# Norm and head scales spread from a step-zero stationary column, and some rounding moved to ScalarE, in a two-layer hybrid diffusion backbone

## What is computed

```python
hx = modulate(rmsnorm(x, g_norm1[l]), mod_x[0], mod_x[1])
px = split_cols(hx @ w_in[l])
...
x = x + mod_x[2] * (jnp.concatenate([m_x, d_x, c_x], axis=-1) @ w_out[l])
...
x = x + mod_x[5] * ffn(modulate(rmsnorm(x, g_norm2[l]), mod_x[3], mod_x[4]))
```

## Time and profile before

| | us |
|---|---|
| median of three runs | 1443.08 |
| the profiled execution, its own time | 1440.16 |
| its span, first to last instruction | 1438.2 |
| TensorE busy | 1376.3 (96%) |
| VectorE busy | 980.4 (68%) |
| ScalarE busy | 629.1 (44%) |
| GpSimd busy | 188.2 (13%) |

### The profile page before, as it was taken

One profiled execution on the slowest core, in us unless ns is written; L12 is line 12 of the kernel. 1 busy time (PEld: TensorE's weight loads), 2 busy tenths in 40 slices (PEclk: granted clock), 3 DMA queues, 4 the chain that ended last, 5 costly groups with the idle time before them and its releaser, 6 DMA issues.

```text
span 1438.2 us, 20655 instructions
## 1 busy us (share of the span) xinstructions
PE 1376.3 (96%) x7782; PEld 1132.2 (79%) x7782; DVE 980.4 (68%) x1470; ACT 629.1 (44%) x993; POOL 188.2 (13%) x136
## 2 busy tenths in 40 slices
PE   6999999989999999999999989798999999999996
PEld 4878787667788888888879887587888888888885
DVE  3756886764644443353468696568898898898896
ACT  3434334642310110010035434646767767777674
POOL 0039980000000000000003960000000000000000
PEclk9999999989999999999999999899999999999998
DMA  9344443412422232232334223439977977977940
GB/s 397 139 176 175 176 176 118 176 59 92 155 105 88 91 115 88 81 110 85 120 118 147 90 87 118 175 133 420 379 284 296 370 278 301 359 297 299 359 163 30
DMA packets 30882, 267.08 MB, mean 186 GB/s; under 512 B 3424, under 2 KB 3552, under 8 KB 4960
## 3 DMA queue, kind: packets, MB, share of 16 engines
q1 hardware_dynamic: 30816, 266.16, 48.6%
HBM read 265.09 MB, written 1.05 MB: 185 GB/s over the span
## 4 chain that ended last, share of the span: by engine, by line
PE 80%; DVE 10%; ACT 4%; issue 3%; DMA 3%; SPq 0%; DVEq 0%; ACTq 0%
PE ps L552 37%; PE ps L1052 17%; PE ps L1072 7%; PE ps L889 3%; PE ps L574 3%; PE ps L739 2%; DMA sb_arena<-mod 2%; PE ps L778 2%; PE ps L797 1%; PE ps L559 1%; DVE sb_egu_lo L2140 1%; DVE sb_h_lo L1622 1%; DVE sb_h_hi L1621 1%; PE ps L788 1%; DVE sb_ew_lo L2152 1%
## 5 line engine op out<-in xcount | busy, mean ns | idle before, releaser
L552 PE MATMUL ps<-sb_h_hi,sb_w_hi 128*128 128x512 f32 (+1 forms) x640 | 241.2, 377 | 2.6 <-DVE sb_w_lo L1636 1.1
L552 PE MATMUL ps<-sb_h_hi,sb_w_lo 128*128 128x512 f32 (+1 forms) x640 | 239.0, 373 | 0.0
L552 PE MATMUL ps<-sb_h_lo,sb_w_hi 128*128 128x512 f32 (+1 forms) x640 | 238.8, 373 | 0.0
L1052 PE MATMUL ps<-sb_egu_lo,sb_h_lo 128*128 128x512 f32 (+1 forms) x384 | 144.2, 376 | 0.0
L552 PEld LDWEIGHTS ps<-sb_h_hi,sb_w_hi 128*128 128x128 f32 x640 | 120.5, 188 | 27.6 <-DVE sb_w_lo L1622 1.8
L552 PEld LDWEIGHTS ps<-sb_h_hi,sb_w_lo 128*128 128x128 f32 x640 | 120.5, 188 | 21.7
L552 PEld LDWEIGHTS ps<-sb_h_lo,sb_w_hi 128*128 128x128 f32 x640 | 120.5, 188 | 20.8
L1621 DVE CAST sb_w_hi<-sb_arena 128x2048 fp32r<-128x2048 f32 (+1 forms) x38 | 45.4, 1196 | 128.7 <-PE ps L552 116.3
L2140 DVE TENSOR_TENSOR sb_egu_lo<-sb_arena,sb_con_r 128x1024 fp32r<-128x1024 f32 x96 | 112.9, 1217 | 13.4 <-ACT sb_con_r L1449 13.4
L2152 DVE TENSOR_TENSOR sb_ew_lo<-sb_arena,sb_ew_hi 128x1024 fp32r<-128x1024 f32 x88 | 107.2, 1218 | 11.5 <-ACT sb_ew_hi L1462 11.5
L2288 POOL TENSOR_SCALAR sb_arena<-sb_arena,sb_small 128x512 f32<-128x512 f32 (+1 forms) x60 | 105.1, 1751 | 5.9
(11 more groups left out here) (348 smaller groups left out, 3020.5 us busy)
## 6 DMA issues: line engine op xcount, KB each, us to landing
sb_arena<-experts SPq DMA_DIRECT2D x90, 1536.0 KB, 8.5
sb_arena<-mod SPq DMA_DIRECT2D x48, 1024.0 KB, 4.9
sb_arena<-in SPq DMA_DIRECT2D x24, 1024.0 KB, 5.2
sb_arena<-gate SPq DMA_DIRECT2D x11, 1024.0 KB, 4.7
sb_arena<-up SPq DMA_DIRECT2D x11, 1024.0 KB, 4.7
sb_arena<-out SPq DMA_DIRECT2D x8, 1024.0 KB, 5.7
sb_arena<-down SPq DMA_DIRECT2D x8, 1024.0 KB, 4.7
sb_arena<-down SPq DMA_DIRECT2D x4, 768.0 KB, 4.1
```

The source lines that it names most:

```text
L552: ins = pe.matmul(o, left[a], right[b], start=(k == first and n == 0), stop=(k == final and n == len(PRODUCTS) - 1))
L1052: ins = pe.matmul(o, x[:, k, :], w[:, span, :], start=(k == 0 and n == 0), stop=(k == KD - 1 and n == 2))
```

## The change

1. The scale is spread without a diagonal. A column of the reciprocals, read 128 times with step zero, is the stationary operand (128x128), and the identity the moving one. One such matmul per block of 128 tokens replaces one with 512 (or 256) columns against ones. VectorE's diagonals fall away in the norms, for the heads and for the convolution.
2. The sum of squares on TensorE waits twice, first for tile 0's sum, then for tile 7's squares; before, both were awaited first. VectorE adds the squares of tile 6 before the residual of tile 7.
3. All four head spreads of a layer stand behind the first two tiles of `part(0)`.
4. In norm B ScalarE makes the leading part of tiles 2 to 7 (`HI_FROM`), each behind the gain and shift of the next tile, and VectorE only subtracts there.
5. `XN_AHEAD` goes from 3 to 2, and the dummy matmuls before the spread of norms B and C from 3 to 1.

```diff
-XN_AHEAD = 3
+XN_AHEAD = 2
+HI_FROM = 2
...
-                pe.wait_ge(*dve_done.at(("ssum", l, which, KD - 2)))
-                pe.wait_ge(*act_done.at(("sq", l, which, KD - 1)))
-                for b in range((T - lo) // P):
-                    for k in (0, KD - 1):
+                for k in (0, KD - 1):
+                    pe.wait_ge(*(act_done.at(("sq", l, which, KD - 1)) if k else dve_done.at(("ssum", l, which, KD - 2))))
+                    for b in range((T - lo) // P):
...
-                pe.wait_ge(*dve_done.at(("ndiag", l, which)))
-                pe.matmul(o[:, 0:T - lo], ones, rstd[:, 0:T - lo], start=True, stop=True).then_inc(*pe_done.tick(("nscale", l, which)))
+                pe.wait_ge(*dve_done.at(("rstd", l, which)))
+                for b in range((T - lo) // P):
+                    ins = pe.matmul(o[:, b * P:(b + 1) * P], nstat[:, 1, b:b + 1].to_broadcast([P, P]), ident, start=True, stop=True)
+                ins.then_inc(*pe_done.tick(("nscale", l, which)))
...
-                part(0, MIX_ORDER[:4])
+                part(0, MIX_ORDER[:2])
+                for h in OUT_ORDER:
+                    spread_scale(l, h)
+                part(0, MIX_ORDER[2:4])
                 if l:
                     turn_modulation(1, MOD_CHUNKS - 2)
-                for h in OUT_ORDER[:2]:
-                    spread_scale(l, h)
                 part(1, MIX_ORDER[:4], (0,))
-                for h in OUT_ORDER[2:]:
-                    spread_scale(l, h)
...
+                    if which and k > HI_FROM:
+                        act.wait_ge(*act_done.at(("h", l, which, k - 1)))
+                        f(h_hi[:, k - 1, :], hT[:, k - 1, :], ACT.Copy).then_inc(*act_done.tick(("h_hi", l, which, k - 1)))
...
+                if which and k >= HI_FROM:
+                    dve.wait_ge(*act_done.at(("h_hi", l, which, k)))
+                    v.tensor_tensor(h_lo[:, k, :], hT[:, k, :], h_hi[:, k, :].bitcast(F32), ALU.subtract)\
+                        .then_inc(*dve_done.tick(("h_split", l, which, k)))
...
-                settled(v.reciprocal(nstat[:, 1, 0:nb], nstat[:, 0, 0:nb]), ("rstd", l, which))
-                v.tensor_tensor(rstd[:, 0:T - lo].rearrange("p (b q) -> p b q", q=P), ident.unsqueeze(1).to_broadcast([P, nb, P]),
-                                nstat[:, 1, 0:nb].unsqueeze(2).to_broadcast([P, nb, P]), ALU.mult)\
-                    .then_inc(*dve_done.tick(("ndiag", l, which)))
+                v.reciprocal(nstat[:, 1, 0:nb], nstat[:, 0, 0:nb]).then_inc(*dve_done.tick(("rstd", l, which)))
...
+                    if m == KD - 1:
+                        sum_squares(*((l, 1) if kind == "y" else (l + 1, 0)), m - 1)
...
-                    if m >= 2:
+                    if 2 <= m < KD - 1:
                         sum_squares(*((l, 1) if kind == "y" else (l + 1, 0)), m - 1)
```

More of the change, by code:

```diff
@@ L75 @@
         ("heads", 0): 0, ("heads", 1): 5, ("scores", 0): 5, ("scores", 1): 0, ("conv", 0): 0, ("conv", 1): 0,
-        ("variance", 0): 6, ("variance", 1): 5, "spread": 3}
+        ("variance", 0): 6, ("variance", 1): 5, "spread": 1}
 MOD_BATCHES = ([(0, 0, 4), (0, 4, 4)] + [(0, i, 2) for i in range(8, 24, 2)] + [(1, i, 2) for i in range(0, 10, 2)]
@@ L283, in build @@
         probT = scratch[:, 4 * T:6 * T].rearrange("p (u b q) -> p u b q", u=2, b=NB)
-        orstd = rows_n[:, 0:NH, :]
-        cdiag = rows_n[:, NH, :]
         h_tok = H[:, KD * SEQ:2 * KD * SEQ].rearrange("p (b n) -> p b n", b=2)
@@ L608, in norm @@
                 spin(o, SPIN["squares", l, which])
-                pe.wait_ge(*dve_done.at(("ssum", l, which, KD - 2)))
-                pe.wait_ge(*act_done.at(("sq", l, which, KD - 1)))
-                for b in range((T - lo) // P):
-                    for k in (0, KD - 1):
+                for k in (0, KD - 1):
+                    pe.wait_ge(*(act_done.at(("sq", l, which, KD - 1)) if k else dve_done.at(("ssum", l, which, KD - 2))))
+                    for b in range((T - lo) // P):
                         ins = pe.matmul(o[:, b:b + 1], squares(l, which)[:, k, b * P:(b + 1) * P], ones[:, 0:1],
-                                        start=(k == 0), stop=(k > 0))
+                                        start=(k == 0 and b == 0), stop=(k > 0 and b == (T - lo) // P - 1))
                 ins.then_inc(*pe_done.tick(("ssq", l, which)))
@@ L864, in conv_spread @@
                 lo = low(l)
-                pe.wait_ge(*dve_done.at(("cdiag", l)))
+                pe.wait_ge(*dve_done.at(("crstd", l)))
                 o = open_bank(("cscale", l))
-                pe.matmul(o[:, lo:T], ones, cdiag[:, lo:T], start=True, stop=True).then_inc(*pe_done.tick(("cscale", l)))
+                for b in range(lo // P, NB):
+                    ins = pe.matmul(o[:, b * P:(b + 1) * P], cstat[:, 1, b:b + 1].to_broadcast([P, P]), ident, start=True, stop=True)
+                ins.then_inc(*pe_done.tick(("cscale", l)))
             def spread_scale(l, h):
                 lo = low(l)
-                pe.wait_ge(*dve_done.at(("odiag", l, h)))
+                pe.wait_ge(*dve_done.at(("orstd", l)))
                 o = open_bank(("oscale", l, h))
-                pe.matmul(o[:, lo:T], ones, orstd[:, h, lo:T], start=True, stop=True).then_inc(*pe_done.tick(("oscale", l, h)))
+                for b in range(lo // P, NB):
+                    ins = pe.matmul(o[:, b * P:(b + 1) * P], stat[:, 3, h * NB + b:h * NB + b + 1].to_broadcast([P, P]), ident,
+                                    start=True, stop=True)
+                ins.then_inc(*pe_done.tick(("oscale", l, h)))
             def output(l):
@@ L1191, in norm @@
                 act.wait_ge(*dve_done.at(("modc" if which else "modc_first", l)))
[L1192 to L1199, removed]
+                for k in range(KD + 1):
+                    if k < KD:
+                        act.wait_ge(*(dve_done.at(("xn", l, which, k)) if k < KD - 1 else dve_drained.at(("nscale", l, which))))
+                        for s in range(2):
+                            a = s * SEQ
+                            ins = f(hT[:, k, a:a + SEQ], squares(l, which)[:, k, a:a + SEQ], ACT.Identity,
+                                    scale=gain[:, l, which, k, s:s + 1], bias=modc[:, l, 24 * which + k, s:s + 1])
+                        ins.then_inc(*act_done.tick(("h", l, which, k)))
+                    if which and k > HI_FROM:
+                        act.wait_ge(*act_done.at(("h", l, which, k - 1)))
+                        f(h_hi[:, k - 1, :], hT[:, k - 1, :], ACT.Copy).then_inc(*act_done.tick(("h_hi", l, which, k - 1)))
                 if (l, which) in MOD_NORM:
@@ L1598, in split_h @@
             def split_h(l, which, k):
-                dve.wait_ge(*act_done.at(("h", l, which, k)))
-                leading_bits(h_hi[:, k, :], h_lo[:, k, :], hT[:, k, :], ("h_split", l, which, k))
+                if which and k >= HI_FROM:
+                    dve.wait_ge(*act_done.at(("h_hi", l, which, k)))
+                    v.tensor_tensor(h_lo[:, k, :], hT[:, k, :], h_hi[:, k, :].bitcast(F32), ALU.subtract)\
+                        .then_inc(*dve_done.tick(("h_split", l, which, k)))
+                else:
+                    dve.wait_ge(*act_done.at(("h", l, which, k)))
+                    leading_bits(h_hi[:, k, :], h_lo[:, k, :], hT[:, k, :], ("h_split", l, which, k))
             def norm_scale(l, which):
@@ L1924, in attention @@
                 dve.wait_ge(*act_done.at(("ostd", l)))
-                nb, r = NB - lo // P, stat[:, 3, :].rearrange("p (h b) -> p h b", h=NH)[:, :, lo // P:NB]
+                r = stat[:, 3, :].rearrange("p (h b) -> p h b", h=NH)[:, :, lo // P:NB]
                 std = stat[:, 2, :].rearrange("p (h b) -> p h b", h=NH)[:, :, lo // P:NB]
[L1927 to L1934, removed]
+                v.reciprocal(r, std).then_inc(*dve_done.tick(("orstd", l)))
+                for h in OUT_ORDER:
+                    head_mix(h)
             def conv_centre(l):
@@ L1943, in conv_diagonal @@
             def conv_diagonal(l):
-                lo, nb = low(l), NB - low(l) // P
+                lo = low(l)
                 dve.wait_ge(*act_drained.at(("cvar", l)))
[L1946 to L1949, removed]
+                v.reciprocal(cstat[:, 1, lo // P:NB], cstat[:, 0, lo // P:NB]).then_inc(*dve_done.tick(("crstd", l)))
             def conv_scale(l):
```

## The result

The changed kernel took 1449.86 us (median of six runs, 1447.27 to 1450.89), the kernel before 1442.91 beside it: ratio 1.0053, 95% interval 1.0042 to 1.0064. It is slower, as forecast, but by 7 us and not by 3.3. Two later measurements gave 1.0031 (1.0013 to 1.0049) and 1.0049 (1.0033 to 1.0064).

What follows compares the result with a forecast made beforehand. The prediction took the kernel as bound by TensorE's chain of waits, chiefly the entry to the dense part. Its terms summed to +3.3 us: 1443.5 profiled, 1446.4 against the median, range 1442.8 to 1450.2.

Steps and rivals of the forecast that it cites:

- The serial ring: Norm B's tile loop: ScalarE's rounding and VectorE's subtraction wait on each other, lap 3.0 us instead of 1.66, +6.8 us.
- Layer 1's output: Layer 1's output projection: diagonals and a wait fall away and the first spread comes earlier, −1.75 us.
- the price of a pass: Spreads on TensorE: a step-zero pass of 128 columns costs 0.111 us at full clock, 0.193 at low clock.
- the rival with 0.193 at any clock: All spreads: step-zero passes cost 0.193 us whatever the clock, +7.6 us in all, 1450.7; chance 0.10.
- The first rival: Norm B's loop: ScalarE and VectorE overlap, TensorE bounds it at T0+16.1 (T0: first normalising), −5.2 us, 1437.9; chance 0.12.
- Clock in that loop: +0.8: Norm B's loop: TensorE, partly idle, may get a lower clock; 0 to 1.7 us, half taken.
- TensorE fills the stage, −0.45: Norm C: its 0.69 us diagonal goes, last tile's squares start later, spread stays 0.9 at full clock; −0.5 to +0.3.
- 8 x 0.193 = 1.54 and the head takes 2.2: Norm B's head: eight low-clock spread passes, no diagonal; 2.2 us instead of 3.47, −1.25.
- Layer 0's output projection: Layer 0's output projection: early spreads and missing diagonals remove TensorE's waits for VectorE, −1.4 us.
- Norm A's end: End of norm A: with two tiles ahead, tile 7 is normalised one 1.66 us lap later, +1.1 us.
- its case in which the rounding slips in first, +1.1: End of norm A: VectorE's rounding precedes GpSimd's clearing, GpSimd ends 0.42 us after it, +1.1 us.
- the other case, GpSimd first: End of norm A: GpSimd's clearing again precedes VectorE's rounding, and everything moves by 1.66 us.

Runs made afterwards that it cites:

- the two edits alone: Kernel before with only two tiles normalised ahead and ScalarE rounding tiles 2 to 7 in norm B: ratio 1.0043 to before, 6.2 us slower.
- both kernels with the longer first dummies: SPIN_FIRST entries 1 and 4 raised to 3 and 7: changed kernel 1.0055; changed kernel with three tiles ahead and three dummies 0.9989.

## Why the prediction was right in direction and wrong in size

Mean of three traces each of the kernel before and of the changed one, place by place. Each number is the difference between the starts (or ends) of the same two instructions:

| place | before | changed | difference | forecast |
|---|---|---|---|---|
| start to first gain of norm A | 37.09 | 37.86 | +0.8 | 0 |
| norm A to its last weight remainder | 19.00 | 20.50 | +1.5 | +1.1 |
| layer 0's projection and mLSTM | 187.81 | 187.16 | −0.7 | 0 |
| convolution and attention, layer 0 | 62.35 | 61.49 | −0.9 | −0.4 |
| output of layer 0, and head of norm B | 58.44 | 56.81 | −1.6 | −2.8 |
| norm B's loop | 16.96 | 23.65 | +6.7 | +6.8 |
| clock in it and the dense part | 346.44 | 346.53 | +0.1 | +0.8 |
| head of norm C and its stretch | 16.00 | 17.05 | +1.1 | −0.45 |
| layer 1's projection and attention | 195.65 | 196.74 | +1.1 | 0 |
| layer 1's output | 15.04 | 13.30 | −1.7 | −1.75 |
| router: row gathering | 5.32 | 6.47 | +1.2 | 0 |
| rest | 476.32 | 476.69 | +0.4 | 0 |
| sum | | | +7.8 | +3.3 |

**Right.** The serial ring was read from the order alone, and its lap came as forecast (2.97 against 3.0). That the order makes it is shown by the runs with three tiles ahead and with VectorE rounding, and by the two edits alone. Layer 1's output came as forecast too, and so did the price of a pass: 0.112 at clock 1.00 (four head spreads), and 1.72/8 = 0.215 at 0.51 in norm B's head where 0.193 was taken; the rival with 0.193 at any clock falls. The first rival falls for the order as it was changed, and comes true with three tiles ahead (loop 16.28, the rival's sum 16.1). The Trainium skill ("Perfetto Trace Analysis", section "Optimizing Scalar/DVE Operations") has it that moving work to ScalarE may make sense where VectorE is saturated; here that paid only once the two lists no longer waited for each other.

**The step that failed is the clock.** The prediction gave it one term, "Clock in that loop: +0.8", because TensorE is half idle there. It cost nothing there: 1.00 in 374 to 380, with 3.32 busy of 6.00, and the loop took 23.65 in the two other traces as well, where its first 3 us ran at 0.57 and 0.51. All other stages were priced as if their clock would not move. In norm C "TensorE fills the stage, −0.45", and in norm B's head "8 x 0.193 = 1.54 and the head takes 2.2". There the work did fall away, and the stage was run at a lower clock instead:

- Norm C's stretch took 7.3 on average for 5.8. Where its clock was 1.00 with the same head (VectorE rounding; three tiles ahead, twice), norm C took 14.9 from the weight remainder to the projection, 15.5 in two traces of before: the forecast gain is there when the clock is.
- Norm B's head took 10.9 for 11.0 from the start of the weight remainder, although its diagonal and four of its six dummy passes were gone; the clock in its last 4 us was 0.57, 0.50 and 0.51. At clock 1.00 the same head took 9.46 (norm C as before; three tiles ahead, second trace), and the old head 10.32 (third trace of before). So at one clock the edits give 0.9 of the 1.4 that were forecast, and the lower clock took even that back.

```profile
360.80:364.80 4.00, 4.00 (x17) 2.02 (x21) 0.87 (x2) 0.26 (x1) 0.00 (x0) 0.71 0.29 121
359.79:363.79 4.00, 4.00 (x22) 3.48 (x26) 0.18 (x2) 0.26 (x1) 0.00 (x0) 0.57 0.39 164
356.70:360.70 4.00, 3.51 (x29) 2.90 (x32) 0.58 (x3) 0.98 (x3) 0.00 (x0) 1.00 0.55 229
```

These rows are the last 4 us of norm B's head before, changed, and with three tiles ahead (second trace). The two places give 1.5 + 1.2 of the 4.5 that are missing. Layer 0's output projection itself, up to that weight remainder, gave its forecast (−1.5 for −1.4). Norm A's end was mis-sized by 0.4 (below).

Places that hold no instruction of the change go with the clock too. The start was late in the two traces of the changed kernel in which the clock of 33 to 37 was 0.62 and 0.57 (+0.8 on average). The experts' first matmuls (+0.9, inside "rest") were told above. Row gathering took 6.3 to 6.6 at a clock of 0.56 to 0.59 and 5.2 to 5.5 at 0.69 to 0.72 (+1.2). Layer 1's projection and attention took 195.0 in all nine traces in which the clock 85 to 100 us behind the projection's start was 1.00, 194.8 to 197.0 in the seven with 0.89, and 198.4 or more in the four with 0.77 (+1.1). The stretch in the first trace of before and in the third of the changed kernel:

```profile
828.70:843.70 15.00, 11.68 (x91) 10.43 (x92) 14.48 (x29) 3.88 (x13) 13.91 (x13) 1.00 0.17 57
834.30:849.30 15.00, 12.22 (x72) 10.89 (x74) 14.42 (x29) 1.76 (x6) 13.91 (x13) 0.77 0.08 32
```

**Not only three traces say so.** For nearly every execution the mean granted clock is on record. Within one kernel the time falls by some 0.8 us for each 0.001 of clock (0.81 over 140 executions of before, 0.86 over 23 of the changed kernel). The mean clock is 0.9832 before and 0.9805 changed; at or below 0.980 lie 8 of the 140 and 14 of the 23. So of 5.9 us between the two means about 2.2 go with the clock. The other 3.7, an estimate, are what the edits cost at one clock; the forecast without its clock term is +2.5.

**Open.** Why the clock falls more often in the changed kernel is not shown. Of the parts that were run alone (rounding with two tiles ahead, norm A's spread, heads and convolution) none of 40 executions lies at or below 0.980; the new heads of norms B and C were never run alone, so they, or the parts together, remain. Norm C is long in four of five traces with its new head, two tiles ahead and one dummy, and 5.8 in all others, with either constant put back; yet putting back the dummies alone did not lower the median. The slow row gathering came in all three traces of the changed kernel and in four others (three tiles ahead, second trace; norm C as before; both kernels with the longer first dummies). Layer 1's attention does not go with the version: the kernel before has a long one in one of three. The −0.7 in layer 0 need not be the change, as 187.16 stands in a trace of before.

## What to carry to other kernels

Before work is moved from one engine to another, follow one lap through both engines' lists: if the receiver's new instruction stands behind something that needs the giver's next one, the lap is the sum of all steps, whatever the busy shares say. One more tile of lead opened such a ring here, and the loop went from 23.6 to 16.3 us. And a microsecond gained by dropping work in a short stage between large products is only a bound: look at the granted clock on both sides of it, in more than one trace, and compare the times of two kernels together with the mean clock of their executions.

## What was not expected

VectorE's rounding of norm A's last tile and GpSimd's clearing started 0.02 apart. GpSimd and then VectorE in order of time:

```profile
50.55 2.66 POOL L2276 MEMSET sb_arena<- 64x3072 f32 x1 [50.11 <-ACT sb_H L1201]
...
50.53 2.97 DVE L1630 CAST sb_h_hi<-sb_H 128x512 fp32r<-128x512 f32 x1
```

The rounding is recorded as the first, and took 2.97 in place of 0.42, to 0.29 behind the end of the clearing; so it is in all nine traces with two tiles ahead. The prediction took its case in which the rounding slips in first, +1.1. By its effect it is the other case, GpSimd first, with everything 1.66 later; the clearing took 2.66 in place of 2.82, which leaves the measured +1.5. The Trainium skill ("SBUF — State Buffer", section "Who interferes with whom") says that between VectorE's two-port modes and GpSimd whoever issues first holds the shared ports; the full block agrees, the order at 0.02 us does not, unless the record of a start is no finer than that.

The granted clock did not follow TensorE's busy share: 1.00 with 3.32 busy of 6.00 in the loop, 0.64 with 9.00 of 9.00 in norm C. And it is not a property of the instructions: the same 32 row-gathering matmuls, 20.23 to 20.26 behind the same weight remainder in every trace, took 5.2 to 6.6.
